# Two homes for the turned inner tile of four feed-forward stages, the turn moved into the step's last chunk, loops written out, and blanked rotary key tiles

## The reference

```python
def swiglu(x, w_gu, w_down):                      # ffn1, ffn2: width 2816
    gate, up = jnp.split(x @ w_gu, 2, axis=-1)
    return (jax.nn.silu(gate) * up) @ w_down

def sq_relu_mlp(h, w_in, w_out):                  # mlp0, mlp1: width 4096
    return jnp.square(jax.nn.relu(h @ w_in)) @ w_out

def mla_mixer(h, cos, sin, w_dkv, g_q, g_kv, w_uq, w_ukv, w_o):
    ...
    q_pe = apply_rope(q[..., MLA_NOPE:], cos, sin)          # 64 numbers a head
    k_pe = apply_rope(k_pe, cos, sin)                       # 64 numbers, one key for all 8 heads
    q = jnp.concatenate([q[..., :MLA_NOPE], q_pe], axis=-1) # 128 + 64
    k = jnp.concatenate([kv[..., :MLA_NOPE], jnp.broadcast_to(k_pe, (B, S, MLA_HEADS, MLA_ROPE))], axis=-1)
    v = kv[..., MLA_NOPE:]
    o = blocked_causal_softmax_attn(q, k, v, (MLA_NOPE + MLA_ROPE) ** -0.5)
    return o.reshape(B, S, MLA_HEADS * MLA_V) @ w_o
```

## Time and profile before

| | |
|---|---|
| median of 3 runs | 1402.88 us (1402.73 to 1404.42) |
| the profiled execution | 1400.49 us, its span 1398.7 us, 16769 instructions |
| PE busy | 1306.8 us, 93% of the span, 6146 matmuls |
| DVE, ACT busy | 759.0 us (54%), 652.4 us (47%) |
| mean granted clock of PE | 0.977 |
| DMA | 220.24 MB, 157 GB/s |
| chain that ended last | PE 84%, DVE 6%, ACT 6%, issue 2% |

### The profile page before, as it was taken

The page is one execution under the profiler, slowest core; times in us unless marked ns, Lnnn a source line. Parts: engine busy times, 40 slices in busy tenths (PEclk is TensorE's granted clock), DMA queues, the critical chain, the costliest instruction groups (busy, mean ns, idle before and its releaser), DMA issues.

```text
span 1398.7 us, 16769 instructions
## 1 busy us (share of the span) xinstructions
PE 1306.8 (93%) x6146; PEld 1077.0 (77%) x6146; DVE 759.0 (54%) x1073; ACT 652.4 (47%) x832; POOL 12.3 (1%) x17
## 2 busy tenths in 40 slices
PE   6999989988989999998999899999899898999995
PEld 4888877867878788887777778888788776888884
DVE  5555447856474554547635665444544545654553
ACT  5444445553443444436833554444455644544431
POOL 0000000001000000000000000000000000000000
PEclk9999999988999999999989999999999999999998
DMA  6755536531343555544512345444544222455520
GB/s 248 268 193 181 184 115 234 195 123 61 130 156 106 204 180 190 192 138 150 200 70 105 106 147 215 180 182 147 188 178 177 91 90 90 177 205 183 196 95 30
DMA packets 37936, 220.24 MB, mean 157 GB/s; under 512 B 4453, under 2 KB 4469, under 8 KB 22272
## 3 DMA queue, kind: packets, MB, share of 16 engines
q1 hardware_dynamic: 36544, 214.26, 43.2%
q0 software_dynamic: 1056, 4.80, 0.9%
q10 hardware_dynamic: 288, 0.54, 0.1%
HBM read 218.51 MB, written 1.07 MB: 157 GB/s over the span
## 4 chain that ended last, share of the span: by engine, by line
PE 84%; DVE 6%; ACT 6%; issue 2%; DMA 0%; DVEq 0%; SPq 0%; ACTq 0%
PE ps L380 26%; PE ps L382 25%; PE ps L381 25%; DVE wlo L360 3%; ACT whi L352 3%; PE ps L1161 2%; PE ps L578 1%; PE ps L1181 1%; PE ps L414 1%; PE ps L1170 1%; PE ps L825 1%; ACT lg L1218 1%; PE ps L1121 0%; DMA gain<-gains 0%; ACT xt_h L424 0%
## 5 line engine op out<-in xcount | busy, mean ns | idle before, releaser
L360 DVE TENSOR_TENSOR wlo<-w_raw,whi 128x2048 fp32r<-128x2048 f32 (+4 forms) x247 | 469.0, 1904 | 461.0 <-ACT whi L352 460.5
L352 ACT ACTIVATE whi<-w_raw 128x2048 fp32r<-128x2048 f32 (+4 forms) x247 | 394.8, 1604 | 483.3 <-PE ps L382 481.3
L380 PE MATMUL ps<-whi,xt_h 128*128 128x512 f32 (+3 forms) x1040 | 414.1, 398 | 15.1 <-ACT whi L352 5.4
L382 PE MATMUL ps<-whi,xt_l 128*128 128x512 f32 (+3 forms) x1040 | 406.1, 390 | 0.0
L381 PE MATMUL ps<-wlo,xt_h 128*128 128x512 f32 (+3 forms) x1040 | 405.4, 390 | 0.0
L380 PE MATMUL ps<-whi,ot_h 128*128 128x512 f32 x594 | 235.9, 397 | 16.2 <-DVE ot_l L682 8.9
L380 PEld LDWEIGHTS ps<-whi,xt_h 128*128 128x128 f32 x1040 | 197.5, 190 | 59.7 <-ACT whi L352 11.6
L382 PE MATMUL ps<-whi,ot_l 128*128 128x512 f32 x594 | 233.7, 393 | 0.0
L381 PE MATMUL ps<-wlo,ot_h 128*128 128x512 f32 x594 | 233.4, 393 | 0.0
L382 PEld LDWEIGHTS ps<-whi,xt_l 128*128 128x128 f32 x1040 | 197.5, 190 | 40.8
L381 PEld LDWEIGHTS ps<-wlo,xt_h 128*128 128x128 f32 x1040 | 198.0, 190 | 37.3
(11 more groups left out here) (164 smaller groups left out, 762.6 us busy)
## 6 DMA issues: line engine op xcount, KB each, us to landing
w_raw<-ffn_mid SPq DMA_DIRECT2D x80, 768.0 KB, 4.1
w_raw<-mlp_mid SPq DMA_DIRECT2D x56, 1024.0 KB, 4.8
w_raw<-w_qkv SPq DMA_DIRECT2D x12, 1024.0 KB, 4.9
w_raw<-w_sb_qkv SPq DMA_DIRECT2D x12, 1024.0 KB, 4.8
w_raw<-w_xkv SPq DMA_DIRECT2D x8, 1024.0 KB, 4.9
w_raw<-ffn_first SPq DMA_DIRECT2D x8, 512.0 KB, 5.1
w_raw<-w_gate_b SPq DMA_DIRECT2D x4, 1024.0 KB, 4.8
w_raw<-w_gate_a SPq DMA_DIRECT2D x4, 1024.0 KB, 4.8
```

The lines of the kernel that those rows point to most:

```text
L352: nc.scalar.activation(whi[:, s, 0:tiles * width], w_raw[:, s, 0:tiles * width], ACT.Copy).then_inc(w_hi, 1)
L360: nc.vector.tensor_tensor(wlo[:, s, 0:tiles * width], w_raw[:, s, 0:tiles * width], whi[:, s, 0:tiles * width].bitcast(F32), ALU.subtract) ...
L380: nc.tensor.matmul(acc, hi, whi[:, s, c], start=start, stop=False)
L382: return nc.tensor.matmul(acc, lo, whi[:, s, c], start=False, stop=stop)
```

## The change

1. `ot_h` and `ot_l` now hold two homes of the turned tile, slots 0 to `hk` - 1 and `hk` to 2 `hk` - 1, used in turn (`hidden_at`).
2. The turn of step i + 1's tile is moved from the head of step i + 1 into the last chunk of step i, behind the chunk's first down tile. ACT and DVE copy it between their splits for the third and the fourth chunk. The first turn stays where it was, in step 1 before the second chunk. The turn ahead of the tail is gone as a piece of its own, since it now lies in the last step.
3. The loops are written out, so every wait has a constant value.
4. The rotary key goes to two tiles: slot 4 of `pet` has it in rows 0 to 63 and zeros below, slot 5 zeros above and the key in rows 64 to 127. The scores' second product then takes all 128 rows, for even heads with slot 4 and for odd heads with slot 5. DVE writes the zeros at the start of the program.

```diff
-        pet = sb("pet", [P, 5, S])
+        pet = sb("pet", [P, 6, S])
...
-        def load_chunk(sp, n, r=0):
+        def load_chunk(sp, n):
...
+            def hidden_at(self, i):
+                return self.hk * (i % 2)
...
-            def down(self, pe, s, pos, js, first, final):
+            def down(self, pe, i, s, pos, js, final):
                 for a, j in enumerate(js):
                     k, block = (j % self.hk, j // self.hk) if final else (j // NB, j % NB)
+                    at = self.hidden_at(i) + k
                     for t in range(NT):
-                        last = mm3(bankD[t][block], ot_h[:, k, t * P:(t + 1) * P],
-                                   ot_l[:, k, t * P:(t + 1) * P], s, pos + a, TW,
-                                   first and k == 0, final and k == self.hk - 1)
+                        last = mm3(bankD[t][block], ot_h[:, at, t * P:(t + 1) * P],
+                                   ot_l[:, at, t * P:(t + 1) * P], s, pos + a, TW,
+                                   i == 0 and k == 0, final and k == self.hk - 1)
...
-            def step_tensor(self, pe, i, n, r=0, first=False):
-                if not first:
-                    self.turn(pe, i)
+            def step_tensor(self, pe, i, n):
                 for c in range(4):
-                    if first and c == 1:
-                        self.turn(pe, i)
-                    take_chunk(pe, n + c, r)
+                    if i == 1 and c == 1:
+                        self.turn(pe, 1)
+                    take_chunk(pe, n + c)
...
                     if downs:
                         if downs[0] == 0:
                             pe.wait_ge(self.hid_lo, i)
-                        last = self.down(pe, slot_of(n + c), len(ups), downs, first, False)
+                        if c == 3:
+                            self.down(pe, i - 1, slot_of(n + c), 0, downs[:1], False)
+                            self.turn(pe, i + 1)
+                            last = self.down(pe, i - 1, slot_of(n + c), 1, downs[1:], False)
+                        else:
+                            last = self.down(pe, i - 1, slot_of(n + c), len(ups), downs, False)
...
-                self.step_tensor(pe, 1, self.n0 + 4, first=True)
-                with pe.Fori(0, self.steps - 2) as r:
-                    self.step_tensor(pe, r + 2, self.n0 + 8, r)
-                self.turn(pe, self.steps)
+                for i in range(1, self.steps):
+                    self.step_tensor(pe, i, self.n0 + 4 * i)
                 pe.wait_ge(self.hid_lo, self.steps)
...
-            def step_scalar(self, act, i, n, r=0):
-                self.turned_scalar(act, i)
-                next_hi(act, n, r)
-                next_hi(act, n + 1, r)
+            def step_scalar(self, act, i, n):
+                next_hi(act, n)
+                if i == 1:
+                    self.turned_scalar(act, 1)
+                next_hi(act, n + 1)
                 self.take_up_scalar(act, i)
-                next_hi(act, n + 2, r)
-                next_hi(act, n + 3, r)
+                next_hi(act, n + 2)
+                self.turned_scalar(act, i + 1)
+                next_hi(act, n + 3)
...
                         if unit.kind == "dkv":
-                            last = nc.scalar.activation(pet[:, 4, s], bank[:, 2], ACT.Copy)
+                            nc.scalar.activation(pet[0:ROPE, 4, s], bank[0:ROPE, 2], ACT.Copy)
+                            last = nc.scalar.activation(pet[ROPE:P, 5, s], bank[ROPE:P, 2], ACT.Copy)
...
                             qk=[(qt[:, hd, s], kt[:, hd, 0:keys]),
-                                (pet[half, hd // 2, s], pet[half, 4, 0:keys])],
+                                (pet[:, hd // 2, s], pet[:, 4 + hd % 2, 0:keys])],
...
             nc.vector.memset(one[:], 1.0).then_inc(one_set, 1)
+            nc.vector.memset(pet[ROPE:P, 4], 0.0).then_inc(kpe_blank, 1)
+            nc.vector.memset(pet[0:ROPE, 5], 0.0).then_inc(kpe_blank, 1)
```

More of the change, by code:

```diff
@@ L342, in split_hi @@
-        def split_hi(act, n, r=0):
+                sp.wait_ge(w_hi, n - RING + 1)
+                sp.wait_ge(w_lo, n - RING + 1)
+            sp.dma_start(w_raw[:, slot_of(n), 0:tiles * width],
+                         dram[array][k]).then_inc(w_loaded[slot_of(n)], 16)
+        def split_hi(act, n):
             _, _, tiles, width = PLAN[n]
             s = slot_of(n)
-            act.wait_ge(w_loaded[s], r * 16 + 16 * (n // RING + 1))
+            act.wait_ge(w_loaded[s], 16 * (n // RING + 1))
@@ L347, in split_hi, with split_lo @@
             if n - RING in ends:
-                done, value, each = ends[n - RING]
-                act.wait_ge(done, r * each + value)
+                act.wait_ge(*ends[n - RING])
             elif n >= RING:
-                act.wait_ge(w_used, r * RING + (n - RING + 1))
+                act.wait_ge(w_used, n - RING + 1)
             nc.scalar.activation(whi[:, s, 0:tiles * width], w_raw[:, s, 0:tiles * width],
                                  ACT.Copy).then_inc(w_hi, 1)
-        def split_lo(dve, n, r=0):
+        def split_lo(dve, n):
@@ L572, in turn @@
                 pe.wait_ge(self.hidden, i * NT)
-                if not isinstance(i, int) or i > 1:
+                if i > 1:
                     pe.wait_ge(self.hid_lo, i - 1)
@@ L614, in tensor @@
                         norm_tensor(pe, self.following, 0)
-                    used(self.down(pe, slot_of(n + c), 0, list(range(c * each, (c + 1) * each)),
-                                   False, True), n + c)
+                    used(self.down(pe, self.steps - 1, slot_of(n + c), 0, list(range(c * each, (c + 1) * each)),
+                                   True), n + c)
             def take_up_scalar(self, act, i):
@@ L659, in scalar @@
                     tables.bias_scalar(act)
-                with act.Fori(0, self.steps - 2) as r:
-                    self.step_scalar(act, r + 1, self.n0 + 4, r)
-                self.step_scalar(act, self.steps - 1, self.n0 + 4 * (self.steps - 1))
-                self.turned_scalar(act, self.steps)
+                for i in range(1, self.steps):
+                    self.step_scalar(act, i, self.n0 + 4 * i)
                 tail_scalar(act, [self.n0 + 4 * self.steps + c for c in range(4)], self.following)
@@ L668, in hide_vector @@
                     dve.wait_ge(self.acted, i * NT + (t + 1))
-                    if not isinstance(i, int) or i > 0:
+                    if i > 0:
                         dve.wait_ge(self.hid_ps, i)
@@ L704, in vector @@
                     next_lo(dve, self.n0 + c)
-                with dve.Fori(0, self.steps - 2) as r:
-                    self.step_vector(dve, r + 1, self.n0 + 4, r)
-                self.step_vector(dve, self.steps - 1, self.n0 + 4 * (self.steps - 1))
-                self.turned_vector(dve, self.steps)
+                for i in range(1, self.steps):
+                    self.step_vector(dve, i, self.n0 + 4 * i)
                 tail_vector(dve, [self.n0 + 4 * self.steps + c for c in range(4)], self.following,
@@ L717, in sync @@
                         sp.dma_start(h[:, :, TW:D], dram["x"][:, :, TW:D]).then_inc(x_in[1], 16)
-                with sp.Fori(0, self.steps - 1) as r:
-                    for c in range(4):
-                        load_chunk(sp, n + 4 + c, r)
-                for c in range(4):
-                    load_chunk(sp, n + 4 * self.steps + c)
+                for c in range(4, 4 * self.steps + 4):
+                    load_chunk(sp, n + c)
             def gpsimd(self, pool):
@@ L768, in __init__ @@
                         k, n = k + tiles, n + 1
-                    ends[n - 1] = (self.full, NT * (u + 1), 0)
+                    ends[n - 1] = (self.full, NT * (u + 1))
                     if unit.kind in ("qk", "dkv", "pe"):
@@ L1556, in __init__ @@
                 for u in range(NB):
-                    ends[self.chunk(u) + 1] = (self.full, NT * (u + 1), 0)
+                    ends[self.chunk(u) + 1] = (self.full, NT * (u + 1))
             def chunk(self, u):
@@ L1900, in mla_groups @@
                     for i, hd in enumerate(heads):
[L1901 removed]
+                        s = slice(t * P, (t + 1) * P)
                         group.append(dict(
```

66 lines of the change are left out of this document (32 added, 34 removed).

## The result

The changed kernel takes **1381.85 us** (median of 4 runs, 1380.89 to 1383.03); the kernel before, run beside it, 1403.65 us (4 runs, 1402.73 to 1404.90). The ratio is 0.984 with an interval of 0.983 to 0.986, so 21.8 us less. The forecast was 1381.0 us.

The account below looks back on a forecast made before the run. PE holds nearly the whole chain, so only its idle time or overlong matmuls can be won. Terms -12.6 - 7.6 - 2.1 + 0.4 = -21.9 us from the median 1402.88 give 1381.0 us; range 1378 to 1384, 8 in 10 1376 to 1388.

Parts of the forecast that it names:

- The four ends: Ends of ffn1, ffn2, mlp0, mlp1: turning the tile before the tail saves 1.9 + 1.9 + 4.4 + 4.4 = 12.6 us.
- The extra 1.4 us for the slow stretch in each mlp end: Tails of mlp0 and mlp1: 2.4 GHz stays instead of 1.2 GHz, -1.4 us each on top of -3.0.
- The idle time before the residual in mlp0: After mlp0's tail: PE's idle time, 0.24 us, grows to perhaps 0.4 as the tail meets the residual sooner.
- The turn in the steps: Inside the feed-forward steps: the 34 moved turns wait for nothing, 0 us.
- The margin: Hidden rows are finished before the moved turn with 1.17 us to spare in ffn1, 1.15 us in mlp0.
- The loops: The four loops' boundaries: writing them out changes 0 within +-0.2 us.
- +18 packets: Queue for instructions: written-out loops add some 0.3 MB or 18 packets of code to 31, hidden, 0 us.
- The MLA start: First MLA scores, groups 0 and 1 to the turn: 16.7 us becomes 9.1 without height changes, -7.6 us.
- The first rival: Start of the MLA attention: the 1.2 GHz stretch stays after PE's idle 1.49 us; 1386 us, chance 0.27.
- The groups of two heads: MLA attention: four groups each 0.69 us shorter, three on the chain, the fourth lost to a wait; -2.1 us.
- The copies of the rotary key: MLA attention: ACT's one copy becomes two, twice, at most 0.28 us each; +0.4 us, between 0.3 and 0.6.
- its last step: The sum: -21.9 us taken from the median 1402.88, 2.4 us above the profiled 1400.49; 1381.0 us instead of 1378.6.

Follow-up runs that it names:

- e3: The changed kernel without the blanked key tiles (parts 1 to 3 of the change only): 1388.66 us, ratio 0.9898.
- e1: The kernel before with its loops written out and nothing else (part 3 alone): 1401.97 us, ratio 0.9993.
- e5: The changed kernel with the turn six matmuls earlier, ahead of the last chunk's first down tile: 1397.68 us, ratio 0.9965.
- e6: e3 with every second head's two MLA score products in reverse order, halving the height changes and keeping 64-row products: 1383.83 us, ratio 0.9863.
- e10: The changed kernel with the second mixer attention's scores over 128 rows, the neighbouring head blanked with zeros: 1372.45 us, ratio 0.9772.
- e7: The changed kernel with all the mixer's scores over 128 rows, neighbouring head added in, so not the attention's own scores: 1374.51 us.
- e11: e10 plus next scores moved ahead of the transposes of finished rows and one MLA split moved behind group 5: 1370.91 us, ratio 0.9771.
- e2: The kernel before with only the blanked key tiles and full-height second product (part 4 alone): 1395.47 us, ratio 0.9944.
- e4: The changed kernel run and profiled a second time, nothing altered: 1381.71 us, ratio 0.9854.

## Why the prediction was right, and where it was not

- **The four ends**: -12.6 us forecast, 12.63 by the same matmuls in e3 and e1. The extra 1.4 us for the slow stretch in each mlp end was needed: each won 4.5, not 3.0. The idle time before the residual in mlp0, which I let grow from 0.24 us to 0.4, stayed at 0.24. ffn1 won 1.6 to 1.9 for 1.9 in three profiles; behind the wait of 2.96 us there are now 3.4 us at 1.2 GHz in each profile with the moved turn and in none without it.
- **The turn in the steps**: 0 forecast, 0 measured (steps within 0.1 us). The margin was read too large: of the 1.17 and 1.15 us to spare, 0.26 goes into the hand-over from DVE to PE, which e5 brought out, so some 0.86 is left.
- **The loops**: 0 within 0.2 forecast, 0.5 us won at the start of the program, nothing in the steps. +18 packets was exact.
- **The MLA start**: -7.6 forecast, -7.54 measured, 9.14 us for 9.1. The first rival (the stretch stays, 1386) had 0.27; it came in none of the nine profiles with full-height scores. In its argument for the fall I named both idleness and drains. The kernel after has the same idleness of 1.5 us and no slow stretch, so idleness alone does not make it. That it is the changes of height and not the 64 rows rests on e6, one profile.
- **The groups of two heads**: -2.1 forecast, -2.22 measured. The fourth's gain did go into the wait for the exponentials, 1.04 to 1.62 us.
- **The copies of the rotary key** are the step that was mis-sized: +0.4, taken between 0.3 and 0.6, measured 0.8. I priced a new copy at its duration, 0.28 us, at most; but two narrow copies follow each other at 0.27 us with no overlap and the next one another 0.30 behind, where the full copy let the next start after 0.16.
- **What the sum left out** is the rest of the clock: one more slow stretch behind the memory attention in some profiles (matmuls 3400 to 3600 take 45.2 us in seven of the thirteen, 43.6 in the other six), others longer or shorter. By the rows of the table the parts make -12.6 - 7.5 - 2.2 + 0.8 - 0.5 = -22.0, beside 21.8 by the medians. So these others cancel or belong to both kernels. The single profile of before was only a fast one in the mixer, 2.4 us under the median, as the prediction noted in its last step. Taking the median as the base brought the number from 3.3 us off (1378.6) to 0.9 off (1381.0).
- **Luck.** The mechanisms stand term by term, but that the gain came out within 0.1 us of the 21.9 forecast is luck: the copies cost 0.4 us more than forecast and the start of the program won 0.5 that was not, and slow stretches of several us lie differently in every profile.

## What to carry to other kernels

When an engine's dense stretch ends in a short chain through two other engines, move the head of that chain ahead of the last independent work, but read the margin first, with the hand-over between the engines in it (0.26 us here): the same move one tile earlier costs some 0.5 us in nearly every pass. A product of 64 rows among those of 128 is no cheaper and pays 0.20 us a change; zeros in the free rows remove it and may bring the clock back, as in e10. Sum a change over stretches between the same instructions and not over whole spans of two profiles, since a span also holds what the clock did elsewhere.

## What the runs showed of the hardware

- A change between 64-row and 128-row float32 products costs 0.20 us at 128 and at 256 columns.
- Sixteen products that change height each time run at 1.2 GHz for some 10 us, in three of three profiles; with half the changes they don't, in the one profile there is. In the mixer's second attention, whose scores are all of 64 rows, the slow stretch is 13.7 to 30.7 us in ten profiles and 6.8 with full height in three (e7, e10, e11), though the wait ahead is no shorter there (4.57 us, against 4.43 in before and e1). Why 64 rows hold the clock down there and not in e6 is open, and whether it is the rows or the changes of height in the mixer too.
- Behind the wait of 2.79 us for `ot_l` the tails of mlp0 and mlp1 ran at 1.2 GHz for 3.4 us (once 6.8) in all three profiles that have it (before, e1, e2), and in none of the ten without it.
- A matmul that waits for DVE starts 0.26 us behind the end of DVE's instruction (30 of 30 turns in e5). The idle time in the brackets, 0.34 us, is less than the 0.50 us that such a wait costs, since two matmuls without a wait start 0.23 us apart and the first lasts 0.39.
- Two ACT copies from one bank of 64 partitions each take 0.57 us to the next copy, one of 128 partitions 0.16 (e4 and e3).
